# The first block's convolution norm in chunks of channels, with the cross values and the convolution's taps between the heads of its attention

## The reference, cut to what matters

```python
y = rmsnorm(h, norm_mix_g) @ w_in
q = partial_rotary(y[..., 0:512]); k = partial_rotary(y[..., 512:1024]); v = y[..., 1024:1536]
att = dilated_sliding_attention(q, k, v)          # 8 heads of 64
u = a * sigmoid(g)                                # a, g: 512 channels each, from y
u = depthwise_conv(u, 31 taps) + conv_b
conv = silu(layernorm(u, ln_g, ln_b))             # over the 512 channels
h = h + concatenate([att, conv]) @ w_out
...                                               # then the cross attention:
xk = rmsnorm(mem, norm_mem_g) @ w_xk              # 256 memory rows
xv = rmsnorm(mem, norm_mem_g) @ w_xv
```

## Time and profile before

| what | value |
| --- | --- |
| median of 3 runs | 1476.51 us (1467.35 to 1479.66) |
| profiled execution, device time | 1470.95 us |
| its span, first to last instruction | 1468.9 us |
| mean granted clock of TensorE | 0.983 |
| busy shares of the span | PE 95%, PEld 83%, DVE 74%, ACT 57%, POOL 4% |
| chain that ended last, by engine | PE 83%, DVE 13%, ACT 2% |

### The profile page before, as it was taken

The page is one execution under the profiler, slowest core; times in us unless marked ns, Lnnn a source line. Parts: engine busy times, 40 slices in busy tenths (PEclk is TensorE's granted clock), DMA queues, the critical chain, the costliest instruction groups (busy, mean ns, idle before and its releaser), DMA issues.

```text
span 1468.9 us, 21894 instructions
## 1 busy us (share of the span) xinstructions
PE 1394.6 (95%) x8175; PEld 1218.4 (83%) x8175; DVE 1085.5 (74%) x1571; ACT 830.9 (57%) x1150; POOL 56.1 (4%) x60
## 2 busy tenths in 40 slices
PE   5997899999999999999999998998999999999997
PEld 5795587989988988899999997777888888888886
DVE  4989565655557876755555788767898898898896
ACT  4444453543445754444333575445787787787784
POOL 0000000000002130000000013010000000000000
PEclk9999899999999999999999999998999999999999
DMA  8544042555554520455555451117998998988982
GB/s 299 177 151 163 0 145 87 176 196 181 192 189 129 168 77 1 132 166 190 181 192 183 129 184 39 37 65 289 398 352 302 348 340 310 372 318 306 373 317 116
DMA packets 162963, 292.75 MB, mean 199 GB/s; under 512 B 6832, under 2 KB 78924, under 8 KB 162764
## 3 DMA queue, kind: packets, MB, share of 16 engines
q1 hardware_dynamic: 162336, 291.08, 57.4%
q10 hardware_dynamic: 556, 0.67, 0.1%
HBM read 290.69 MB, written 1.05 MB: 199 GB/s over the span
## 4 chain that ended last, share of the span: by engine, by line
PE 83%; DVE 13%; ACT 2%; issue 1%; DMA 1%; ACTq 0%; SPq 0%; POOL 0%; DVEq 0%
PE bank L537 23%; PE bank L539 23%; PE bank L538 23%; DVE weights_split L1915 4%; DVE arena L2100 3%; PE bank L1199 2%; PE bank L1002 1%; PE bank L1274 1%; PE bank L1008 1%; PE bank L993 1%; PE bank L671 1%; PE bank L651 1%; PE bank L1020 1%; PE bank L1251 1%; DMA weights<-in_w_in_dram 1%
## 5 line engine op out<-in xcount | busy, mean ns | idle before, releaser
L1915 DVE TENSOR_TENSOR weights_split<-weights,weights_split 128x1024 fp32r<-128x1024 f32 (+4 forms) x266 | 304.4, 1187 | 168.8 <-ACT weights_split L1427 168.7
L1427 ACT ACTIVATE weights_split<-weights 128x1024 fp32r<-128x1024 f32 (+4 forms) x266 | 258.5, 1022 | 285.9 <-PE bank L539 283.2
L537 PE MATMUL bank<-features_split,weights_split 128*128 128x256 f32 x912 | 263.2, 289 | 15.2 <-DVE features_split L1942 5.4
L538 PE MATMUL bank<-features_split,weights_split 128*128 128x256 f32 x912 | 260.8, 286 | 0.0
L539 PE MATMUL bank<-features_split,weights_split 128*128 128x256 f32 x912 | 260.7, 286 | 0.0
L537 PE MATMUL bank<-weights_split,features_split 128*128 128x512 f32 (+3 forms) x560 | 217.5, 388 | 8.5 <-DVE features_split L1922 3.6
L539 PE MATMUL bank<-weights_split,features_split 128*128 128x512 f32 (+3 forms) x560 | 214.0, 382 | 0.0
L538 PE MATMUL bank<-weights_split,features_split 128*128 128x512 f32 (+3 forms) x560 | 213.8, 382 | 0.0
L537 PEld LDWEIGHTS bank<-features_split,weights_split 128*128 128x128 f32 x912 | 177.7, 195 | 18.8 <-DVE weights_split L1915 6.2
L538 PEld LDWEIGHTS bank<-features_split,weights_split 128*128 128x128 f32 x912 | 177.9, 195 | 0.5
L539 PEld LDWEIGHTS bank<-features_split,weights_split 128*128 128x128 f32 x912 | 177.8, 195 | 0.0
(11 more groups left out here) (374 smaller groups left out, 2250.9 us busy)
## 6 DMA issues: line engine op xcount, KB each, us to landing
weights<-in_moe_gate_dram SPq DMA_DIRECT2D x26, 1024.0 KB, 6.8
weights<-in_moe_up_dram SPq DMA_DIRECT2D x24, 1024.0 KB, 7.0
weights<-in_moe_down_dram SPq DMA_DIRECT2D x24, 1024.0 KB, 7.3
weights<-in_w_in_dram SPq DMA_DIRECT2D x20, 1024.0 KB, 5.2
weights<-in_w_up_dram SPq DMA_DIRECT2D x16, 1024.0 KB, 5.2
weights<-in_w_down_dram SPq DMA_DIRECT2D x16, 1024.0 KB, 4.9
weights<-in_w_out_dram SPq DMA_DIRECT2D x12, 1024.0 KB, 4.9
weights<-in_ffn_gate_dram SPq DMA_DIRECT2D x11, 1024.0 KB, 5.3
```

The costliest lines, as they stand in the source:

```text
L537: pe.matmul(ps, lhs(0), rhs(0), start=start, stop=False, skip_group_check=shared)
L538: pe.matmul(ps, lhs(0), rhs(1), start=False, stop=False, skip_group_check=shared)
L1427: do(act.activation(split_flat(j)[:, 0, part], raw_flat(j)[:, part], ACT.Copy), "hi", j, b)
L1915: do(dve.tensor_tensor(split_flat(j)[:, 1, part], raw_flat(j)[:, part], split_flat(j)[:, 0, part].bitcast(F32), ALU.subtract), "lo", j)
```

## The change

- The cross values are no longer computed ahead of the attention. TensorE does half a slot of them (12 matmuls) in each of the attention's slots 0 to 7, behind the head's own work. The fourth cross key slot moves behind the turns of queries and keys.
- VectorE keeps 13 of the 38 pair-taps and three of the eight `low` ahead of the attention; four pair-taps come ahead of the rotary step, two fewer in the loop before the memory's norm. The other 23 pair-taps and five `low` stand between the steps of the attention: one pair-tap in each slot while the exponentials run, one or two at the slot's end, a `low` in slots 0, 2, 4, 6 and 8.
- ScalarE scales the probabilities (two Copy instructions with a scale for each row), in a new function for this attention alone, and has a `high` ahead of slots 2, 4, 6 and 8, and the cross values' copies behind slots 3, 4, 7 and 8.
- The product with the reciprocal is made chunk by chunk, each `Silu` waits for its own chunk, the split is made in two halves, and TensorE waits for the first half ahead of rows 4 and 5 and for the second ahead of rows 6 and 7.
- A `Silu` of one column stands right behind the root.

```diff
--- before.py
+++ after.py
@@ -704,10 +704,8 @@
                 turn_norm(1)
                 tokens_out("v", HT, 512)
                 pe.wait_ge(*after("ht", 1))
-                for i in range(4):
+                for i in range(3):
                     features_out("xk", MT, "xk", i)
-                for i in range(2):
-                    tokens_out("xv", MT, 512, i)
...
                     mm.then_inc(*cpe.mark("filled", "qkT", b))
+                features_out("xk", MT, "xk", 3)
                 pe.wait_ge(*after("read", "qkT", 3))
                 pe.wait_ge(*after("read", "v", 0, 1))
+                cross_slot = {}
+
+                def cross_values(s):
+                    if s >= 8:
+                        return
+                    i, r, t = s // 4, s // 2 % 2, s % 2
+                    if t == 0:
+                        cross_slot[i, r] = weights("xv")
+                    j, w = cross_slot[i, r]
+                    ps = open_bank("xv", i, t) if r == 0 else bank_of["xv", i, t]
+                    for k in range(4):
+                        mm = matmul3(ps[:, :], lambda z: MT[:, z, 4 * r + k, t * P:(t + 1) * P],
+                                     lambda z: w[:, z, k, :], r == 0 and k == 0, r == 1 and k == 3)
+                    if r == 1:
+                        mm.then_inc(*cpe.mark("filled", "xv", i, t))
+                        cpe.also("slot", j)
+                    elif t == 1:
+                        mm.then_inc(*cpe.mark("slot", j))
...
-                attention(0, AH, scores1, pair_outs("att_o", (), V))
+                attention(0, AH, scores1, pair_outs("att_o", (), V), between=cross_values)
...
-                pe.wait_ge(*after("convT"))
                 for c in range(2):
                     j, w = weights("wout")
                     for t in range(TT):
                         if c == 1 and t == 1:
                             first_half_raw(2)
-                        mixed_rows(c, w, (4, 5, 6, 7), (t,), last=True).then_inc(*cpe.mark("filled", "wout", c, t))
+                        pe.wait_ge(*after("convT", 0))
+                        mixed_rows(c, w, (4, 5), (t,))
+                        pe.wait_ge(*after("convT", 1))
+                        mixed_rows(c, w, (6, 7), (t,), last=True).then_inc(*cpe.mark("filled", "wout", c, t))
                     cpe.also("slot", j)
...
+                def first_attention(heads, ahead, between):
+                    for s in range(heads + 1):
+                        ahead(s)
+                        if s >= 1:
+                            act.wait_ge(*after("pt", s - 1))
+                            if s >= 3:
+                                act.wait_ge(*after("o", s - 3))
+                            do(act.activation(flat(PT[:, (s - 1) % 2]), PT_BANK[(s - 1) % 2][:, 0:TT * S], ACT.Copy),
+                               "pt_copied", s - 1)
+                        if s < heads:
+                            exps(s, False)
+                            act.wait_ge(*after("rden", s))
+                            for t in range(TT):
+                                do(act.activation(PR[:, s % 3, t, :], PR[:, s % 3, t, :], ACT.Copy,
+                                                  scale=RDEN[:, s % 3, t:t + 1]), "probs", s)
+                        between(s)
+
...
-                for i in range(4):
+                for i in range(3):
                     high(1)
                     copy_out(XKT[:, 2 * i:2 * i + 2, :], two(psum("xk", i)), "xk", i)
-                for i in range(2):
-                    high(2)
-                    for t in range(TT):
-                        copy_out(XV[:, t, i * 512:(i + 1) * 512], psum("xv", i, t)[:, :], "xv", i, t)
                 act.wait_ge(*after("heads_selected"))
                 for b in range(4):
                     copy_out(QKT[:, 2 * b:2 * b + 2, :], two(psum("qkT", b)), "qkT", b)
-                attention(0, AH)
+                copy_out(XKT[:, 6:8, :], two(psum("xk", 3)), "xk", 3)
+                high(1)
+
+                def next_slot(s):
+                    if s in (2, 4, 6, 8):
+                        high(1)
+
+                def cross_values(s):
+                    if s in (3, 4, 7, 8):
+                        i, t = s // 4 - (s % 4 == 0), 1 - s % 2
+                        copy_out(XV[:, t, i * 512:(i + 1) * 512], psum("xv", i, t)[:, :], "xv", i, t)
+
+                first_attention(AH, next_slot, cross_values)
 
                 act.wait_ge(*after("read", "cmean"))
                 do(act.activation(SIG[:, :, :], C[:, :, :], ACT.Square), "csq")
                 act.wait_ge(*after("read", "cvar"))
                 do(act.activation(U[:, 0, 0:S], U[:, 0, 0:S], ACT.Sqrt), "csd")
+                do(act.activation(SM[:, 15, 0:1], NHALF[:, 0:1], ACT.Silu))
                 high(1)
-                act.wait_ge(*after("cnormed"))
                 for i in range(4):
+                    act.wait_ge(*after("cnormed", i))
                     do(act.activation(C[:, i, :], C[:, i, :], ACT.Silu, bias=col("conv_ln_b", i),
-                                      scale=col("conv_ln_g", i)), "csilu")
+                                      scale=col("conv_ln_g", i)), "csilu", i)
...
                         rows_norm(1, MEM)
-                    conv_taps(4 if i < 2 else 2)
+                    conv_taps(3 if i < 2 else 2)
                     low(1)
                 turned(1, "norm_mem_g", 0, MT, T1)
+                conv_taps(4)
                 for _ in range(2):
                     low(1)
...
-                for i in range(8):
+                for i in range(3):
                     low(1)
-                    conv_taps(5 if i < 6 else 4)
-                assert taps_done == [TAPS, TAPS]
+                    conv_taps(4)
...
-                    do(dve.tensor_tensor(C[:, :, :], C[:, :, :],
-                                         U[:, 1, 0:S].unsqueeze(1).broadcast_to([P, 4, S]), ALU.mult), "cnormed")
+                    for i in range(4):
+                        do(dve.tensor_tensor(C[:, i, :], C[:, i, :], U[:, 1, 0:S], ALU.mult), "cnormed", i)
 
                 def conv_split():
-                    dve.wait_ge(*after("csilu"))
-                    split(lambda z: CAT[:, z, 4:8, :], C[:, :, :], "convT")
-
-                attention(0, AH, 0.125, flat(logc), outs1)
+                    for p in range(2):
+                        dve.wait_ge(*after("csilu", 2 * p + 1))
+                        split(lambda z: CAT[:, z, 4 + 2 * p:6 + 2 * p, :], C[:, 2 * p:2 * p + 2, :], "convT", p)
+
+                conv_taps(1)
+                for s in range(AH + 2):
+                    if s < AH:
+                        dve.wait_ge(*after("scores", s))
+                        if s >= 3:
+                            dve.wait_ge(*after("pt", s - 3))
+                        do(dve.scalar_tensor_tensor(flat(PR[:, s % 3]), SC_BANK[s % 2][:, :], 0.125, flat(logc),
+                                                    ALU.mult, ALU.add), "scores_read", s)
+                        own()
+                        do(dve.tensor_reduce(NM[:, s % 3, :], PR[:, s % 3], AX.X, ALU.max, negate=True), "negmax", s)
+                        conv_taps(1)
+                        dve.wait_ge(*after("exp", s, 1))
+                        do(dve.reciprocal(RDEN[:, s % 3, :], DEN[:, s % 3, :]), "rden", s)
+                    if s in (0, 2, 4, 6, 8):
+                        low(1)
+                    if s >= 3 and s % 2:
+                        outs1(s - 2)
+                    conv_taps(2 if s % 2 else 1)
+                assert taps_done == [TAPS, TAPS]
                 conv_mean()
                 conv_variance()
                 conv_scaled()
```

## The result

The changed kernel takes 1460.29 us as a median of 20 runs (1457.42 to 1468.45), against 1471.05 for the kernel before (20 runs, 1466.67 to 1479.66): a ratio of 0.9927, 95% interval 0.9909 to 0.9944, or 10.7 us less. The forecast was 10.5 us less, within 1%. As a median it was 1466, which started from the 1476.51 of three runs; 20 runs put the kernel before 5.5 us lower, and the median forecast is too high by about as much.

The account below looks back on a forecast made before the run. TensorE, busy 95% of the span, bounds the kernel; only its gaps around the first attention can pay. Earlier mean -8.6, its slow clock +1.6, norm -3.5: -10.5 us, from 1476.51 to a median of 1466, range 1453 to 1477.

Parts of the forecast that it names:

- Before the attention: Stretch up to the softmax: with work moved out, VectorE takes first scores at 112.9 instead of 140.9, 28.0 us earlier.
- The attention: First attention, from first scores to mean: nearly balanced engines, 50.7 us, so the mean starts at 163.6 instead of 172.2.
- 5.84 + 1.2: VectorE's slot 0: 5.84 us of an even slot, plus 1.2 for exponentials late behind ScalarE's table load.
- my bounds of 0.39 and 0.52: ScalarE's scaling of probabilities in the attention: 0.39 to 0.52 us each, the first taken.
- late exponentials in slots 2 and 4: ScalarE's split stands ahead of copy and exponentials in these attention slots: +0.5 us in all.
- who is in front: Attention slots: VectorE expected in front, with TensorE at about 5.4 us per slot, 5.6 at most.
- The mean: Channel mean after the attention: starts 8.6 us earlier but runs at the 1.2 GHz level, +1.6, bounds 0 and 3.4.
- The norm: Convolution's norm and split: TensorE's 2.10 us wait and the slow clock behind it go, -3.5 us; bounds nothing or -4.2.
- The sum: Whole stage: -8.6 + 1.6 - 3.5 = -10.5 us, the shift lasting to the end.
- The slow clock in the attention: Rival: attention slots at 1.2 GHz, 5.3 us more each; two slots cancel the gain; chance 0.15.
- Handoffs: Rival: ScalarE late by 0.5 us per attention slot, convolution's split still awaited; gain only 4.5, 1472; chance 0.16.
- Rival 1: Slower by the clock: attention slots at 1.2 GHz, all eight making it 32 us slower (1498); chance 0.15.

Follow-up runs that it names:

- e7: Changed kernel with a one-column exponential on ScalarE ahead of its copy of the fourth cross key bank, so the table loads in a wait; ratio to before 0.9887.
- e5: Changed kernel with three pair-taps moved from slots 8 and 9 into VectorE's wait for the first scores; ratio to before 0.9876.
- e1: Kernel before with only the norm's part of the change (chunked products, Silu behind the root, split in halves); ratio to before 0.9988.
- e12: Changed kernel with 6 idle matmuls of ones in TensorE's wait for the last tap; ratio to before 0.9919.
- e2: Changed kernel with the norm's part undone, leaving the interleaving alone; ratio to before 0.9930.
- e11: Changed kernel without the one-column Silu behind the root, so its table loads behind the weight split again; ratio to before 0.9935.
- e3: Changed kernel with cross values, fourth cross key slot and all eight weight splits back ahead of the attention, taps still spread over it; ratio to before 1.0015.
- e4: Changed kernel with all taps ahead of the attention, cross values and five weight splits still between the heads; ratio to before 0.9992.
- e6: Changed kernel with 13 idle matmuls of ones between TensorE's last head and its wait for the last tap; ratio to before 0.9924.
- e8: Changed kernel with the first 12 output-matrix matmuls moved ahead of the mean and the next 12 ahead of the variance; ratio to before 0.9911.

## Why the prediction was right

**Before the attention.** Forecast -28.0 us for the first scores, measured 111.68 - 140.86 = -29.2. Of this, 1.30 was there at the rotary step: 0.86 ahead of any changed instruction, 0.24 more at the first weights behind the norm (71.58 instead of 72.68), which fits the two pair-taps that left the loop ahead of the memory's norm and which I had taken to be hidden, and the rest from a lower clock behind that wait that ended sooner in this execution. From the rotary step on it is 22.52 instead of 50.40, **-27.9**.

**The attention.** Forecast 50.7 us, measured 50.12. VectorE's sum by instructions held: slot 0 in 7.01 (forecast 5.84 + 1.2), and e7 shows the 1.2 to be the table's load. A scaling of 256 columns took 0.46 (two in 0.91), between my bounds of 0.39 and 0.52. The 0.5 us for late exponentials in slots 2 and 4 came out smaller: slot 2 took 5.97 and slot 4 5.70, against 5.84 without them. What I had wrong is who is in front: TensorE's slot is 5.60 us, the upper bound of my sum and not the 5.4 that I took from the starts, because the 12 cross matmuls take 2.95 from start to start of their neighbours and not 12 x 0.23 = 2.76: 0.1 more at the first and at the change behind the last. VectorE's slots average 5.5, so from 127 us on TensorE is busy for 27.90 of 27.90 us, and VectorE waits for it at 144.92. It changed the sum by nothing, since the two are equal within 0.1 a slot. At the end VectorE is last again, with the taps (e5).

**The mean.** Forecast -8.6 for its start; counted from the rotary step it is 72.64 - 81.71 = -9.07. Of this, 1.3 us is slow clock that the profiled execution of the kernel before had in its attention and e1, with the same code there, had not (81.71 against 80.38); against e1 the mean comes 7.7 earlier. The forecast was counted from that same execution, so it took this piece in without my knowing it. Forecast +1.6 for its clock; e12 measured +2.36. The step was right and its size low, as the first weights behind the mean are slow too, which I had named in the bound only. The row shows it: no matmul from 160.0 to 161.8 and the granted clock at 0.50, then nine matmuls at 1.2 GHz. The Trainium skill's rule (TensorE: Matmul & The Clock Gate, "What's actually happening") that the lower level is the default and activity lifts it agrees with this: in e12 2.9 us of idle matmuls kept 2.4 GHz.

**The norm.** Forecast -3.5; e1 measured -4.01 in the clock's favour and e2 -2.42 without. The halves were ready when TensorE came. In the changed kernel the end of the first half's split and the first of the last weights are:

```profile
177.45 0.69 DVE L1967 TENSOR_TENSOR features_split<-arena,features_split 128x512 fp32r<-128x512 f32 x1
```

```profile
178.68 0.39 PE L537 MATMUL bank<-weights_split,features_split 128*128 128x512 f32 x1
```

That is a slack of 0.5 us (178.68 - 178.14) where I had 0.9, and in e11 the 1.3 us of the load used it up and left a wait of 0.41.

**The sum.** With the mean's start and its clock the terms add up to the stage: -9.07 + 2.36 - 4.01 = -10.72, measured -10.73. They are not independent. In the changed kernel the norm's part is worth 2.42 and the interleaving alone 8.31 (118.93 - 110.62), which gives the same sum; 1.6 us move from one to the other with the clock behind the wait of 2.10. The mechanism held term by term, but that the sum is within 0.3 us is partly luck: the terms are off by -0.5, +0.8 and -0.5, and whole executions put the gain only between 8.2 and 13.4 us.

**The load of a table.** The Trainium skill (ScalarE: Activation LUTs, "What ACT_TABLE_LOAD costs") gives 2.66 us for a switch, 1.28 of loading and 1.38 of draining. The rows here show the 1.28 and 0.04 around it (111.11 + 2.00 = 113.11 to 113.14, and 114.42 to 114.43), and e7, which takes the switch out of the chain, gains 1.30 in the slot. The measurement decides: 1.3 us is the price in this place.

**Rivals.** The slow clock in the attention didn't come: the granted clock was 1.00 from 112 to 155 us, though TensorE waited 1.03 and 1.23 us in slots 1 and 2. e3 and e4 show the mechanism to be real where one engine is left without work. Handoffs took nothing: slots 1 and 3 were 0.2 us shorter than my sum, slot 5 0.1 longer. Rival 1's price for all eight slots was added up wrongly: 42 - 10.5 = 32 us slower than 1476.5 is 1508 and not 1498; the forecast doesn't use it. Not tried: the cross values in fewer, larger pieces, which would show how long a pause the clock stands inside the attention.

## What to carry to other kernels

Before an interleaving, sum each engine's instructions per step; the move pays when both engines have room in the same place, and either half alone may be worth nothing. The first place to look afterwards is a pair of waits at the two ends of the new stage: work that one end waits for may fit into the idle time of the other (three pair-taps here: 3.1 us by the earlier mean and 2.4 by its clock). Judge parts of a few microseconds between two marks of the trace close around the change, since clock changes elsewhere move whole executions by more.

## What the runs showed of the hardware

- A matmul of 256 float32 columns whose operands are not in the rounded format ran as two records of 0.23 us each (26 for 13 in e6). A matmul of 512 columns in the rounded format also takes 0.23, so a column of this kind costs four times as much.
- TensorE kept the clock of 2.4 GHz over waits of 1.03, 1.23 and 1.19 us with work between them, and lost it over the one of 3.06 us ahead of the mean: from 155.0 to 161.8 it had 2.55 us of work, and the granted clock was 0.50 from 160.0 on. In e8, behind the same work, a wait of 1.68 us there was enough. Behind continuous work a wait of 2.10 us at the last weights cost the clock in the kernel before and not in e2, and one of 2.17 did in e8. The norm's part, which takes such a wait away, was worth 4.0 us in the first case and 2.4 in the second.
